# A hybrid attention, recurrence and expert layer: fewer steps in its mixing stage, inverse updates on half the columns, and another item kept in SBUF

## The reference, cut to what matters

```python
z = rmsnorm(x) @ w_in                     # 1024 -> 2056 + 1792 columns
# 8 "fox" heads: softmax attention with a forget bias
log_f = log_sigmoid(ff + fox_f_bias)      # ff: 8 columns of z, one per head
logit = q @ k.T / sqrt(64) + c[t] - c[s]  # c = cumsum(log_f)
# 8 "rwkv" heads: a recurrence over time
S_t = S_{t-1} diag(w_t) + (S_{t-1} a_t) b_t^T + v_t k_t^T ;  y_t = S_t r_t
mean = jnp.mean(y, -1); var = jnp.mean((y - mean)**2, -1)   # per head of 64
y = (y - mean) * rsqrt(var + GN_EPS) * ln_w + ln_b
x = x + concat([fox_out, rwkv_out]) @ w_out
# experts: the 4 best of 32 for each token, w_gu 1024 x 2048, w_down 1024 x 1024
x = x + moe_ffn(rmsnorm(x), ...)
x = x + sigmoid(rmsnorm(x) @ w_ple_gate) * (p @ w_ple_proj)
return rmsnorm(x)
```

## Time and profile before

| | before |
|---|---|
| median of 3 timed runs | 1192.65 us (1192.38 to 1194.75) |
| the profiled execution, time | 1191.82 us |
| its span, first to last instruction | 1190.0 us |
| PE busy | 1135.6 us (95%) |
| DVE, ACT busy | 283.4 us (24%), 173.1 us (15%) |
| moved by DMA | 434.76 MB, mean 365 GB/s |
| granted clock of PE | 0.999 |
| chain that ended last | DMA 43%, PE 40%, DVE 1% |

### The profile page before, as it was taken

The page is one execution under the profiler, slowest core; times in us unless marked ns, Lnnn a source line. Parts: engine busy times, 40 slices in busy tenths (PEclk is TensorE's granted clock), DMA queues, the critical chain, the costliest instruction groups (busy, mean ns, idle before and its releaser), DMA issues.

```text
span 1190.0 us, 16884 instructions
## 1 busy us (share of the span) xinstructions
PE 1135.6 (95%) x7064; PEld 478.2 (40%) x7064; DVE 283.4 (24%) x578; ACT 173.1 (15%) x319; POOL 0.2 (0%) x4
## 2 busy tenths in 40 slices
PE   7999999999999999999999999999999999999997
PEld 6888866433333333333333333333333333333334
DVE  2455634421112111111121111111111111111123
ACT  3323422210001000001100000000000000000015
POOL 0000000000000000000000000000000000000000
PEclk9999999999999999999999999999999999999999
DMA  9752126599999999989999999999999999999970
GB/s 374 323 213 74 32 113 239 225 362 426 426 428 429 427 427 430 428 332 404 430 426 430 428 428 428 428 429 428 427 429 427 428 429 428 429 428 427 428 329 35
DMA packets 34026, 434.76 MB, mean 365 GB/s; under 512 B 4032, under 2 KB 4288, under 8 KB 6976
## 3 DMA queue, kind: packets, MB, share of 16 engines
q1 hardware_dynamic: 33984, 434.13, 87.0%
HBM read 433.06 MB, written 1.05 MB: 365 GB/s over the span
## 4 chain that ended last, share of the span: by engine, by line
DMA 43%; PE 40%; DVE 1%; issue 0%; ACT 0%; SPq 0%; DVEq 0%
DMA ring<-in_we 43%; PE PS L924 27%; PE PS L1028 2%; PE PS L748 2%; PE PS L872 2%; PE PS L887 2%; PE PS L941 1%; PE PS L879 1%; PE PS L975 0%; PE PS L810 0%; PE PS L950 0%; PE PS L543 0%; PE PS L815 0%; PE PS L895 0%; PE PS L771 0%
## 5 line engine op out<-in xcount | busy, mean ns | idle before, releaser
L924 PE MATMUL PS<-ring,FV 128*64 128x512 f32 x2276 | 509.3, 596 | 25.0 <-DMA ring<-in_we 24.9
L924 PEld LDWEIGHTS PS<-ring,FV 128*64 128x64 f32 x2276 | 156.2, 137 | 358.9 <-issue 299.8
L924 PE MATMUL PS<-B,FV 128*64 128x512 f32 x772 | 175.1, 595 | 8.7 <-DMA B<-in_we 8.7
L924 PEld LDWEIGHTS PS<-B,FV 128*64 128x64 f32 x772 | 53.2, 137 | 115.6 <-issue 98.9
L531 PE MATMUL PS<-hT,ring 128*128 128x256 f32 x416 | 93.0, 382 | 1.0 <-ACT hT L1081 0.7
L531 PEld LDWEIGHTS PS<-hT,ring 128*128 128x128 f32 x416 | 78.1, 190 | 12.3 <-ACT hT L1081 0.9
L1568 DVE TENSOR_SCALAR rz<-con,lora 128x64 f32<-128x64 f32 x30 | 7.6, 255 | 305.3 <-PE PS L924 305.3
L1650 DVE TENSOR_SCALAR hT<-PS 128x512 f32<-128x512 f32 x32 | 22.1, 692 | 184.5 <-PE PS L924 184.5
L1335 DVE TENSOR_TENSOR FV<-PS,prm 128x512 f32<-128x512 f32 x32 | 22.1, 692 | 183.8 <-PE PS L879 183.8
L1240 ACT ACTIVATE FV<-PS 128x512 f32<-128x512 f32 x32 | 19.1, 597 | 297.0 <-PE PS L975 297.0
L872 PE MATMUL PS<-xq,rz 128*64 128x512 f32 x256 | 62.0, 605 | 0.0
(11 more groups left out here) (273 smaller groups left out, 680.2 us busy)
## 6 DMA issues: line engine op xcount, KB each, us to landing
ring<-in_we SPq DMA_DIRECT2D x135, 2048.0 KB, 24.4
B<-in_we SPq DMA_DIRECT2D x48, 2048.0 KB, 29.8
ring<-in_wz SPq DMA_DIRECT2D x7, 2048.0 KB, 22.8
ring<-in_we SPq DMA_DIRECT2D x14, 1024.0 KB, 7.8
ring<-in_wo SPq DMA_DIRECT2D x2, 2048.0 KB, 7.8
ring<-in_wgate SPq DMA_DIRECT2D x2, 2048.0 KB, 38.8
stash<-in_we SPq DMA_DIRECT2D x1, 2048.0 KB, 13.1
xq<-in_x SPq DMA_DIRECT2D x2, 512.0 KB, 5.7
```

The lines of the kernel that those rows point to most:

```text
L924: mm = pe.matmul(PS[64 * h:64 * h + 64, bank_, :], lhs(4 * (q % 2) + k), early[u] if u < units else w[:, k, h, :], start=(first and k == 0 ...
```

## The change

- **The kept item** is item 17 instead of 11. The items 11 to 16 are now loaded whole with `in_turn`, by one item outside the loop, a new loop of two times two items, and one item more; the kept item and `wproj` follow.
- **bp** has no step of its own: its product rides beside q4, and ACT copies it after the q4 product. x0 waits for that copy.
- **ff** is multiplied with 32 stationary columns in four column groups at once, one k block in each; ACT copies the four partial results (128x256), a product with the new constant `fold8` adds them (`ff0`), and ACT adds the bias (`ffh`). These stand after t1.
- **Centring** moves into v: DVE makes `centre` = eye - 1/64 once, and the v product beside q2 uses it in place of `eye`. `mean` and `cent` are gone; `vsq` waits for the copy of y.
- **Levels**: the t products have 32 moving columns in place of 64, those that the level's mask leaves (every other run of 2^k), both results in one bank each (6 and 7); DVE adds 512 columns in place of 1024. The q product's copy goes to tile 13 (levels 1 to 4). `q k` now waits for DVE's `tt k-1` instead of `t k-1`; t k waits for nothing on DVE any more.
- **The start**: SP waits until the first half of x has landed before it issues the first weight load.

```diff
@@ MIX_ORDER
-MIX_ORDER = [("z", 18), ("bp", 0), ("z", 19), ("ma", 0), ("z", 20), ("aa", 0), ("z", 21), ("z", 22),
-             ("q", 1), ("z", 26), ("qsq", 0), ("ffa", 0), ("ffe", 0), ("t", 1), ("fc", 0), ("qss", 0),
+MIX_ORDER = [("z", 18), ("z", 19), ("ma", 0), ("z", 20), ("aa", 0), ("z", 21), ("z", 22),
+             ("q", 1), ("z", 26), ("qsq", 0), ("t", 1), ("ff", 0), ("ffa", 0), ("ffe", 0), ("qss", 0), ("fc", 0),
...
+        def q_at(k):
+            return 13 if k < 5 else 4
+
+        def level_half(i, k, bit):
+            return b16(i).rearrange("p g (a s b) -> p g a s b", s=2, b=1 << k)[:, :, :, bit, :]
...
-        NEARLY, KEPT_ITEM = len(early), 11
+        NEARLY, KEPT_ITEM = len(early), 17
...
+            sp.wait_ge(s_x[0], 16)
             for n in range(NSLOT):
                 piece(n, t[f"wz{n}"], ZP[n][1])
...
             in_turn(2 * EARLY + 2, False, range(3))
+            in_turn(2 * EARLY + 3, True)
+            with sp.Fori(EARLY, KEPT_ITEM // 2 - 2) as p:
+                in_turn(2 * p + 4, False)
+                in_turn(2 * p + 5, True)
+            in_turn(KEPT_ITEM - 1, False)
             in_turn(KEPT_ITEM, True, kept_item=True)
...
-            with sp.Fori(EARLY, pairs) as p:
+            with sp.Fori(KEPT_ITEM // 2 - 1, pairs) as p:
...
-                        mm = pe.matmul(PS[0:NHEAD, z_bank(n), 0:SEQ], wff[:, k, :], hT[:, k, :], **flags)
+                        rows = slice(NE * (k % 4), NE * (k % 4) + NE)
+                        four = wff[:, k // 4 * 4:k // 4 * 4 + 4, :].rearrange("p k n -> p (k n)")
+                        mm = pe.matmul(PS[rows, z_bank(n), 0:SEQ], four, hT[:, k, :], start=(k < 4), stop=(k >= 4))
...
-                if kind == "bp":
-                    pe.wait_ge(s_dve, dve_at["tildes"])
-                    fin(per_head((6, blocks(4), eye, 0)), "bp0")
...
+                elif kind == "ff":
+                    pe.wait_ge(s_act, act_at[f"z{NZ}"])
+                    fin(pe.matmul(PS[0:NHEAD, z_bank(NZ), SEQ:2 * SEQ], c_("fold8"), ff4, start=True, stop=True), "ff0")
...
-                        pe.wait_ge(s_dve, dve_at[f"t{k - 1}"])
+                        pe.wait_ge(s_dve, dve_at[f"tt{k - 1}"])
...
-                        beside = ((2, blocks(2), eye, 0),)
+                        beside = ((2, blocks(2), centred, 0),)
...
+                    elif k == 4:
+                        pe.wait_ge(s_act, act_at["kp"])
+                        pe.wait_ge(s_dve, dve_at["tt3"])
+                        beside = ((4, blocks(4), eye, 0),)
...
-                    fin(per_head((6, blocks(14), blocks(4), 1), (4, blocks(4), blocks(14), 0)), f"t{k}")
+                    fin(per_head((6, blocks(14), columns(q_at(k), k, 0), 1), (7, blocks(q_at(k)), columns(14, k, 1), 0), n=CH // 2), f"t{k}")
...
-            pe.wait_ge(s_act, act_at[f"y{NC - 1}"])
-            sums(4, b4(8), "mean")
...
+                    elif n == 4:
+                        fin(act.activation(flat(6), two(4), ACT.Copy), "bp")
...
+            def update(i, k, bit, b):
+                part = level_half(i, k, bit)
+                return tt(part, bank(b).rearrange("p (g a b) -> p g a b", g=16, b=1 << k), part, ALU.add)
...
-                        fin(tt(flat(8), two(6), flat(8), ALU.add), f"t{n}")
-                    fin(tt(flat(14), two(4), flat(14), ALU.add), f"tt{n}")
+                        fin(update(8, n, 0, 6), f"t{n}")
+                    fin(update(14, n, 1, 7), f"tt{n}")
...
-            pe_done("mean")
             v.memset(LG[:, :, NE:36], PAD)
-            fin(v.scalar_tensor_tensor(out=flat(8), in0=two(4), scalar=-1.0 / HD, in1=flat(8),
-                                       op0=ALU.mult, op1=ALU.add), "cent")
+            act_done(f"y{NC - 1}")
```

More of the change, by code:

```diff
@@ L581, in eye, with centred @@
                 return prm[rows, PARAM["ident"][0] + rows.start:PARAM["ident"][0] + rows.stop]
+            def centred(rows, g):
+                return centre[rows, :]
             def blocks(i):
@@ L590, in _, with columns @@
             sums(6, b4(7), "bn")
+            def columns(i, k, bit):
+                return lambda rows, g: level_half(i, k, bit)[rows, g]
             def ar(s):
@@ L1139, in _ @@
                     z(n)
+                elif kind == "ff":
+                    pe_done("ff0")
+                    fin(act.activation(tmp8[:, 0, :], PS[0:NHEAD, z_bank(NZ), SEQ:2 * SEQ], ACT.Identity,
+                                       bias=p_("fb")[0:NHEAD, :]), "ffh")
                 elif kind == "ffe":
@@ L1148, in _ @@
                     fin(act.activation(FG[:, :, :], FG[:, :, :], ACT.Tanh, scale=0.5), "fg")
-                elif kind == "bp":
-                    pe_done("bp0")
-                    fin(act.activation(flat(6), two(6), ACT.Copy), "bp")
                 elif kind in ("qss", "kss"):
@@ L1160, in _ @@
                     pe_done(f"q{n}")
-                    fin(act.activation(flat(4), two(6), ACT.Copy), f"q{n}")
+                    fin(act.activation(flat(q_at(n)), two(6), ACT.Copy), f"q{n}")
                     if n == 1:
```

39 lines of the change are left out of this document (19 added, 20 removed).

## The result

The changed kernel takes 1186.35 us (median of 8 runs, 1184.8 to 1189.86) against 1193.79 us of the kernel before on the same chip (8 runs, 1191.2 to 1194.93): a ratio of 0.9945, 95% interval 0.9933 to 0.9957. That is 7.4 us less in the medians and 6.6 by the ratio, where 10.6 were forecast; 1182.0 us was the forecast, 1186 the upper end of the range. Its profiled execution has a span of 1184.5 us (1190.0 before), so 5.5 us less.

What follows compares the result with a forecast made beforehand. The DMA stream, standing still once, and PE's time up to the first item were taken to bound the kernel. Stream -7.8 and mixing stage -2.8 gave -10.6 us: 1192.65 to 1182.0 us, range 1178.5 to 1186.

Steps and rivals of the forecast that it cites:

- The stream: DMA stream around items 10 to 12: moving the kept item to 17 removes 6.8 + 1.0 us idle, -7.8 us.
- Item 12's and item 17's margins: Stream at items 12 and 17: loads are issued in time, with 1.9 and 4.9 us to spare, so no new gap.
- rival 3: Stream: a gap of the same size stays, at item 12 or 17; only -2.8 us, 1189.9 us; chance 0.10.
- rival 4: Stream: SP can't keep it fed at items 11/12 and 17/18; slower, 1196.7 us; chance 0.02.
- bp: Mixing stage: bp's own step goes, its product beside q4 costs nothing measurable; -2.0 us.
- mean: Mixing stage: without mean, w_out starts earlier but waits for DVE's last attention step; -1.2 us.
- the start: Start of mixing stage: x alone on the queues ends 0.28 us of idle; -0.3 us, bounds -0.9 and +1.0.
- q4 and kln: Level behind t4: the copy of bp delays kln past PE's own work; +0.6 us.
- The levels from q1 to the z half behind q2: ACT's chain makes PE wait 2.9 us; z half starts 12.5 us after q1's start; +0.6 us, ff's saving lost.
- The halved columns: t products in the levels: 1.9 us each instead of 2.02, four of five on the path; -0.5 us.
- Rival 1: t products: moving columns set the pace in 64x64 blocks, saving 3.3 us, not 0.5; 1179.2 us; chance 0.15.
- Rival 2: Mixing stage gives nothing (late weights, or ACT waits twice as long); -7.8 us alone, 1184.9 us; chance 0.08.

Runs made afterwards that it cites:

- experiment 1: Kernel before with only the kept item moved to 17 and the loads of items 11 to 16 that go with it: 1184.83 us, ratio 0.9927.
- experiment 9: experiment 6 plus 32 small unread products at the start over all four quadrants, shifting the code half a piece: 1179.38 us, ratio 0.9877.
- experiment 6: Changed kernel with the second half of w_out loaded later and one ScalarE table for logarithm and exponential: 1181.67 us, ratio 0.9916.
- experiment 10: Changed kernel with only 32 small unread products added at the start, shifting the code by half a piece: 1183.81 us, ratio 0.9919.
- experiment 3: Changed kernel with the load of the second half of w_out issued after block z23 instead of z21: 1186.77 us, ratio 0.9942.
- experiment 4: experiment 3 plus nine unread products on TensorE behind q2, filling its wait for ScalarE: 1184.31 us, ratio 0.9928.
- experiment 2: Changed kernel with the kept item back at 11, so the mixing stage's changes alone: 1195.54 us, ratio 1.0025.
- the first kernel of experiment 8: experiment 7 plus 64 small unread products at the start, shifting the code by a whole piece: 1198.88 us, ratio 1.0048.
- experiment 5: Changed kernel with one ScalarE table for logarithm and exponential in place of two: 1186.78 us, ratio 0.9945.
- the second kernel of 11: experiment 9 with full 64 columns in the level products and VectorE's additions: 1183.22 us, ratio 0.9917.
- experiment 7: Changed kernel with the old ff product back (eight products of 8 columns, ahead of t1): 1185.91 us, ratio 0.9938.
- the first kernel of 11: Changed kernel with full 64 columns in the level products and VectorE's additions: 1191.61 us, ratio 0.9988.

## Why the prediction was right or wrong

**The stream: right.** -7.8 forecast, 8.3 in the two traces, 8.7 in the medians of the kept item alone. By traces it varies: first item and late piece give 7.1 us in experiment 1, 7.3 and 7.4 in experiments 9 and 6, 8.6 in experiment 10. Item 12's and item 17's margins held: no stretch of 100 us from 280 to 1080 is under 427 GB/s, and the lowest of 5 us is 406, at `wproj` (720 to 725 us). One part was off without cost: between 530 and 770 us the chain waits for the DMA once, from 669 to 695.5 us, for the last piece ahead of the kept item, so of the 4 us that TensorE was to have in hand there none was left; the stream didn't stop for it. Rivals 3 and 4 fall.

**bp, mean: right; the start: luck.** The ff product came 2.80 us earlier, of which 0.60 were there at the first z product (forecast 0.3, bound 0.9) and 2.2 stand between the two, where bp was (forecast 2.0). The 0.60 are no measure of the new start. Without the small products at the start, the eight traces with the new start have their first z product at 13.14 (the changed kernel's, the earliest) to 14.17 us, 13.8 in the middle, and the two with the old start at 13.74 and 14.07. A gain of 0.1 is all that they suggest, a tenth of their spread. `w_out` follows the last attention product after 1.45 us where it took 2.64 before: 1.19 for the mean, 1.2 forecast.

**q4 and kln: right.** A wait of 0.65 us behind t4, 0.6 forecast.

**The levels from q1 to the z half behind q2: the step that failed.** The prediction added up ScalarE's chain and came to 12.5 us from the start of q1, with a wait of 2.9 us. The wait came (2.75), but the stretch took 119.47 - 104.49 = 14.98 (q1 starts 2.03 ahead of the ff product). Where the fetch was out of the way (experiment 3) it was 117.50 - 104.95 = 12.55. The arithmetic held to 0.05 us; missing was a term that isn't in the diff, the 2.21 us in which t1's code was not there. It could have been suspected: before, the 3.6 us of the ff product lay over this fetch (it crossed at 110.7, the product ran from 109.32 to 112.87), and the change put t1, 128 passes of 16 ns, there in its place.

**No term for the clock: the second step that failed.** I took the durations of the rows before as given. But the prediction itself forecast 2.9 us of idle TensorE, where the kernel before never stood still for more than 0.3 in this stretch. The granted clock halved behind it: 1.7 us on the z half in the changed kernel, 4.5 in experiment 3, nothing where the wait was filled or taken away (experiments 4 and 6). The second stretch, ahead of the first item, cost 1.4 us more in this execution (from +1.38 at 230 us to +2.80). It comes and goes with the execution, in the mixing stage of the kernel before too (experiment 1), so it isn't the change's.

**The halved columns: too high by 0.4.** A t product takes 2.00 us from row to row, 2.02 or 2.03 before, where I took 1.9; four of them give 0.1, not 0.5. The earlier trace rows pointed the right way: the moving columns don't set the pace. Whether the loading of weights does, as I took it, or a fixed cost of each pass, no run tells, and my half of 0.11 was too fine a reading. By the Trainium skill, TensorEngine Tiling (Array Packing), "Instruction Overhead", the levels give nothing; the trace agrees with its 0.02 to 0.04 us a product. Rival 1 falls.

The sum again, in us: -0.6 - 2.2 + 0.6 (ScalarE's chain) + 2.2 (fetch) + 0.3 (chain, the rest) + 1.7 (clock) + 0.5 (q4, kln, and the rows between) - 1.2 + 1.5 (second clock stretch, and the rows between) = +2.8, as measured. The first and the last of these terms belong to this pair of executions; without them 1.9 are left, and the medians of experiment 2 say +2.5. Rival 2, "the mixing stage gives nothing", came nearest in time (1184.9), but for other reasons than the ones that it names: neither late weights nor a wait of ScalarE twice as long. I gave it 0.08. The whole mixing stage was forecast as a sum of work removed; it lies on the path, but TensorE's own work was not its only limit.

## What to carry to other kernels

A term "so much work removed from TensorE" holds only as far as code and clock follow: when a long product ahead of many short ones goes, ask whether the fetch of the next piece of code had been hiding behind it, and whether a bulk transfer runs at that moment. Where your own forecast says that TensorE will wait where it never did before, put a price on the rows behind the wait. If a kernel's time moves by 1 to 3 us with an edit that shouldn't matter, move its code by half a piece (128 instructions here) before you explain it. Before you credit an edit with 1 or 2 us from one pair of traces, see how far the same code differs between traces (here 1 us at the first z product and 1.4 us ahead of the first item). And compare variants of an edit only with their idle time of the "issue" kind beside the time.

## What the runs showed of the hardware

- TensorE's code comes in pieces of 16 KB, and one t product is 256 instructions in 2.0 us (128 passes and as many loads). Where a piece is late TensorE stands still for 0.2 to 2.2 us, shown as "issue", and goes on 2.4 to 2.8 us after the piece has crossed the queue. The Trainium skill, Runtime: NRT & Kernel Launch, "Instruction fetch mechanics", gives blocks of 16 KiB with 256 instructions, as the counts here do, and calls the crossing of a boundary mostly hidden. In the kernel before it was hidden at every boundary of the levels; after the change it cost up to 4.3 us in one kernel (1.14, 1.48 and 1.69 in the first kernel of experiment 8).
- Half clock in the levels came behind idle times of 1.94 to 2.76 us in the changed kernel and in experiments 2, 3 and 5, and was gone with them in 4, 6 and 9. But idle time alone doesn't decide: behind 1.1 us it came in experiment 10 and not in the second kernel of 11, behind 1.2 to 1.4 us not in 6 and 7, and the first kernel of 11 fell to half clock in t1, behind two idle times of 1.06 us, but had 3.23 us of it behind q2 and kept 1.00. Ahead of the first item all kernels have the same work and the same 0.85 us wait, and the clock fell in the executions of some (the changed one, experiments 1, 3, 4 and 9, the first kernels of 8 and 11) and not of others. What decides within this span stays open.
